# A planned single-core kernel: another order for the opening, and a last block that is scaled at eviction and fed from eleven weight-tile places

## The chip, the cores and the metric

The kernel runs on one core of one Trainium2 chip. The metric is the device time of one execution in microseconds (us), lower is better; the figure of a kernel is the median of its runs.

## The reference

Two model layers follow each other on 512 tokens of width 1024 (16 meta tokens stand ahead of them in the first), all in float32.

```python
# first_block: h = [meta; x], 528 rows
a = rmsnorm(h); aq, ak, av, rq, rf, ri, rg = split(a @ w_in)
att = diff_attention(aq, ak, av)    # rope, 4 heads, softmax(p0) - lam * softmax(p1), rmsnorm
rec = hgrn2(rq, rf, ri, rg)         # gated linear recurrence in chunks, rmsnorm, * silu(rg)
h = (h + [att, rec] @ w_out)[16:]
h = h + peer_ffn(rmsnorm(h))        # per token: 8 heads x top 16 of 16384 experts;
                                    # y = sum_k gelu(u[e_k] . x) * gate_k * v[e_k]
x = rmsnorm(h)
# second_block
q, k, v, z_a, u_b, v_b, z_b, g_a, g_b = split(rmsnorm(x) @ w_in_2)
y_a = stick_breaking_attention(q, k, v) * silu(z_a)      # 8 heads of 64
y_b = spatial_gating(gelu(u_b), gelu(v_b)) * silu(z_b)
x = x + (sigmoid(g_a) * (y_a @ w_up_a) + sigmoid(g_b) * (y_b @ w_up_b)) @ w_out_2
return rmsnorm(x)
```

The expert table is 16384 rows of 2048 floats (u and v of an expert together).

## The kernel before, in words

The tokens are four blocks of 128 rows, in partitions. Everything that any engine does is one list of steps, PLAN, made by make_plan from tables of rows written out by hand; each engine walks the same list and issues its own part of every step, so the order within an engine is the order of the list. Steps are named by a short name, the block or group of blocks, and a tile number: rf, rq, ak, aq, av, ri, rg are the seven projections of the first layer (four weight tiles each), n0/norm1 the norm and its transposes, fs/f/f2/lx/ly/lm/kd/ke/kdt/st the recurrence, us/ue/uw/ut/uv one attention head (scores, exponentials, weights, transposes, values), r1..r3 and a1..a3 the norm and transposes of the recurrent and the attention result, out the output projection. xn/xt/x2/x3, wq/sc/s1 and tk choose the experts. q2, k2, v2, vb, ub, zb, za, ga, gb, ua, ud, wo are the projections of the second layer, zs/zd/ze/zt/zv one unit of its attention, ln/l2/sg/yb the spatial gate, ya/yo/mt the transposes ahead of ua and wo, n1/m1/n2/n3 the two norms between the layers, fin/fd/store the last norm and the store.

Three parts follow each other. The opening (opening_rows, L155, and opening_keys) takes block 0 through the first layer's mixing up to its first experts. The middle is 256 ticks: POOL gathers 512 groups of 128 expert rows (1 MB each) into a ring of eight places, uv_rows; DVE multiplies them with the tokens (L1835), ACT takes gelu, DVE builds the weights (L1844, L1845) and PE adds the rows up in two PSUM banks, psum_y ("py"), the two halves of the tokens in output partitions 0-63 and 64-127. All other work of blocks 1 to 3 of the first layer and blocks 0 to 2 of the second is spread over these ticks. Behind the last tick last_rows (L245) takes block 3 through the second layer alone.

Weights come as tiles of 128 x 1024 floats (512 KB) in four places, wbuf. SP loads tile n into place n % 4 as soon as tile n - 4 was used (load_tile, L747 on); wherever a step uses a tile, SP's list has its load. PE matmuls are f32, and each is two instructions in the trace. Two rings of three PSUM banks, psum_a ("pa", emptied by ACT, semaphores a_full and a_free) and psum_b ("pb", emptied by DVE, b_full and b_free), take the results: cols_tile writes a projection transposed, rows_tile adds four tiles (16 instructions of 512 columns in the trace) into one bank per block. For block 0, rows_tile has a second bank for the 16 meta rows (`ps[0:NM, :]`), with as many instructions.

Around the last block: take_sums copies the two psum_y banks to h1 (L1851), n1 and m1 scale by the first layer's last norm (square, Ln and Exp on ACT, L1988 on DVE), n2 scales by the second layer's norm the same way, n3 transposes the rows (L895) and multiplies the columns by the norm's weights (L1589). Only then do q2 and k2 start, by cols_tile (L861). In opening_rows av stands behind us(0), rg behind us(2), and the eight steps of out at the very end:

```python
rows += [us(0), av, [("uw", b, 0)], [("ut", b, 0)], us(1), [("kdt", b), ("uw", b, 1), ("st", b)]]
rows += [[("uv", b, 0), ("ut", b, 1)], us(2), rg, [("r1", b), ("uw", b, 2)], [("uv", b, 1), ("ut", b, 2)], us(3)]
```

## Time and profile before

| | |
|---|---|
| median of 3 runs | 1992.65 us (1985.96 to 1992.9) |
| the profiled execution, its own time | 1989.25 us |
| its span, first to last instruction | 1987.5 us |
| busy in the span: PE, DVE, ACT, POOL | 1665.7, 1328.0, 653.7, 592.4 us |
| mean granted TensorE clock | 0.932 of 2.4 GHz |
| moved by DMA | 729.05 MB, mean 367 GB/s |

A row of instructions gives the start, the busy time (or the stretch from first to last start and end), engine, line, operation, what is written from what is read, and, in brackets, the idle time ahead of it with what ended it.

### The profile page before, as it was taken

How to read it: one execution, taken by the hardware profiler on the slowest of the kernel's cores; microseconds unless marked ns; L12 is line 12 of the kernel's file. 1: busy time of each engine (PE TensorE's matmuls, PEld its weight loads, DVE VectorE, ACT ScalarE, POOL GpSimd, SP SyncE). 2: the span in 40 equal slices, each digit the busy share in tenths (PEclk: the TensorE clock that was granted, in tenths of full speed). 3: DMA queues.
4: the chain of work that ended last, by engine and by line, in shares of the span. 5: the costliest groups of instructions: out<-in, count | busy, mean ns of one | idle time of the engine just before them, and what ended most of it. 6: DMA issues, size and time to landing. Idle time of an engine off the chain costs nothing.

```text
span 1987.5 us, 19846 instructions
## 1 busy us (share of the span) xinstructions
PE 1665.7 (84%) x6622; PEld 812.3 (41%) x6622; DVE 1328.0 (67%) x3461; ACT 653.7 (33%) x1219; POOL 592.4 (30%) x516
## 2 busy tenths in 40 slices
PE   7987798778898998788589999789986877876997
PEld 7445463225454443335145434333334222222653
DVE  4337787976788888875876578977656679644231
ACT  3123433323343265222231233511221246211361
POOL 0002233433232343533433233433323334421000
PEclk9988998889999998889899998899998988999999
DMA  7439999999999999999999999999999999998665
GB/s 219 133 120 367 417 417 417 421 417 417 397 402 356 352 413 360 353 420 414 421 416 417 418 416 372 356 411 418 419 403 362 417 412 409 419 417 344 212 222 180
DMA packets 130021, 729.05 MB, mean 367 GB/s; under 512 B 15600, under 2 KB 17264, under 8 KB 64384
## 3 DMA queue, kind: packets, MB, share of 16 engines
q0 software_dynamic: 73728, 536.90, 66.2%
q1 hardware_dynamic: 56192, 190.88, 25.8%
q8 instruction: 53, 0.87, 0.2%
q14 instruction: 48, 0.39, 0.1%
HBM read 725.63 MB, written 2.10 MB: 366 GB/s over the span
## 4 chain that ended last, share of the span: by engine, by line
PE 48%; DMA 23%; DVE 17%; ACT 5%; issue 5%; POOL 1%; POOLq 0%; DVEq 0%; SPq 0%; ACTq 0%
PE pa L861 27%; DMA uv_rows<-in_peer_uv,small 13%; PE py L861 12%; DMA wbuf<-in_wt 9%; PE pb L861 8%; DVE uv_rows L1835 6%; ACT area L1223 2%; ACT L1217 2%; POOL uv_rows L2025 1%; DVE tk L1845 1%; DVE area L1899 1%; DVE tk L1844 1%; DVE small L1822 1%; ACT small L1223 1%; DVE small L1740 1%
## 5 line engine op out<-in xcount | busy, mean ns | idle before, releaser
L2025 POOL DMA_INDIRECT uv_rows<-in_peer_uv,small x512 | 592.2, 1157 | 1214.5 <-PE py L861 968.3
L1835 DVE CUSTOM_DVE_ANT_0 uv_rows<-uv_rows,xrep 128x1024 f32<-128x1024 f32 x512 | 615.6, 1223 | 224.4 <-DMA uv_rows<-in_peer_uv,small 221.5
L861 PE MATMUL py<-uv_rows,tk 128*64 128x512 f32 x2048 | 568.9, 682 | 204.0 <-DVE tk L1845 203.3
L861 PE MATMUL pa<-wbuf,area 128*128 128x512 f32 (+2 forms) x864 | 383.8, 586 | 29.1 <-DMA wbuf<-in_wt 27.2
L1223 ACT ACTIVATE small<-small 128x2 f32<-128x2 f32 (+4 forms) x324 | 69.2, 214 | 847.4 <-DVE small L1835 823.6
L861 PEld LDWEIGHTS py<-uv_rows,tk 128*64 128x64 f32 x2048 | 136.5, 149 | 510.9 <-DVE tk L1845 277.6
L1217 ACT ACT_TABLE_LOAD x250 | 320.8, 1283 | 5.4 <-DVE small L1931 1.0
L861 PE MATMUL pa<-area,wbuf 128*128 128x128 f32 (+2 forms) x1408 | 249.3, 335 | 21.3 <-issue 11.1
L861 PEld LDWEIGHTS pa<-wbuf,area 128*128 128x128 f32 (+1 forms) x864 | 149.6, 189 | 254.5 <-issue 201.6
L861 PEld LDWEIGHTS pa<-area,wbuf 128*128 128x128 f32 x1408 | 215.9, 198 | 75.6 <-issue 41.7
L1223 ACT ACTIVATE area<-pa 128x512 f32<-128x512 f32 (+7 forms) x234 | 91.9, 409 | 310.4 <-PE pa L861 290.1
L861 PE MATMUL pb<-wbuf,area 128*128 128x512 f32 x352 | 164.8, 615 | 12.3 <-DMA wbuf<-in_wt 7.4
L1844 DVE TENSOR_TENSOR tk<-small 128x2 f32<-128x2 f32 x256 | 41.4, 162 | 104.0 <-issue 50.2
L861 PEld LDWEIGHTS pb<-wbuf,area 128*128 128x128 f32 x352 | 64.9, 194 | 111.6 <-issue 91.3
L861 PE MATMUL pa<-area 128*128 128x64 f32 (+7 forms) x392 | 77.9, 331 | 6.7 <-ACT area L1223 5.0
L1845 DVE TENSOR_TENSOR tk<-small,tk 128x128 f32<-128x128 f32 x256 | 74.8, 292 | 8.9
L861 PE MATMUL pb<-area 128*128 128x128 f32 (+7 forms) x434 | 77.4, 319 | 1.1 <-ACT area L1223 1.1
L1223 ACT ACTIVATE area<-area 128x512 f32<-128x512 f32 (+3 forms) x104 | 67.5, 655 | 26.8 <-DVE area L1631 18.8
L861 PEld LDWEIGHTS pa<-area 128*128 128x128 f32 (+2 forms) x392 | 54.1, 201 | 39.4 <-issue 23.0
L861 PEld LDWEIGHTS pa<-xnT,wbuf 128*128 128x128 f32 x512 | 59.3, 192 | 21.1 <-issue 16.5
L861 PE MATMUL pa<-xnT,wbuf 128*128 128x128 f32 x512 | 63.5, 280 | 2.2 <-DVE xnT L1589 1.1
L861 PEld LDWEIGHTS pb<-area 128*128 128x128 f32 (+2 forms) x434 | 54.9, 192 | 19.2 <-issue 13.9
(218 smaller groups left out, 1065.7 us busy)
## 6 DMA issues: line engine op xcount, KB each, us to landing
wbuf<-in_wt SPq DMA_DIRECT2D x336, 512.0 KB, 8.0
uv_rows<-in_peer_uv,small POOLq DMA_INDIRECT x512, 13.1
wbuf<-in_skT SPq DMA_DIRECT2D x11, 256.0 KB, 7.5
h<-in_x SPq DMA_DIRECT2D x4, 512.0 KB, 10.8
out<-h SPq DMA_DIRECT2D x4, 512.0 KB, 5.5
an<-in_x SPq DMA_DIRECT2D x3, 512.0 KB, 5.8
area<-in_finw SPq DMA_DIRECT2D x2, 512.0 KB, 10.0
area<-in_masks SPq DMA_DIRECT2D x1, 512.0 KB, 6.8
```

The costliest lines, as they stand in the source:

```text
L861: return nc.tensor.matmul(o, l, r, start=start, stop=stop, skip_group_check=True)
L1217: nc.scalar.preload_act_table_set(TABLES[func])
L1223: return nc.scalar.activation(dst, src, func, **more)
L1740: last = V.tensor_reduce(mx[:, q, part:part + 1], psum_a[(first + part) % RA][:, 0:nk - lo], AXX, ALU.max)
L1822: V.tensor_scalar(gate[to, cols], gexps[tok, g % 2, s_::TG], gsum[tok, g % 2, 1:2], None, ALU.mult)
L1835: last = V.tensor_tensor_reduce(uv_rows[:, n % RING, 0:D], uv_rows[:, n % RING, 0:D], xrep[:, b % 2, n % TG, :], 1.0, 0.0, ALU.mult, ALU.a ...
L1844: step(V.tensor_tensor(wcol[:, k % 2, :], dots[:, at:at + BATCH], gate[:, col:col + BATCH], ALU.mult))
L1845: V.tensor_tensor(mix_w[k % 2], token_mask.unsqueeze(1).broadcast_to([P, BATCH, TOK]), wcol[:, k % 2, :].unsqueeze(2).broadcast_to([P, BAT ...
L1899: step(V.tensor_tensor_scan(rcs[:, 0:wide][:, ::-1], seg2[:, 0:wide], soft[:, 0:wide][:, ::-1], 0.0, ALU.mult, ALU.add))
L2025: nc.gpsimd.indirect_dma_start(uv_rows[:, n % RING, :], None, t["peer_uv"], bass.IndirectOffsetOnAxis(ap=expert_ids[:, c:c + 1].bitcast(U3 ...
```

## The change

In the opening, the tiles of ri and av are taken in turn, and the meta rows of both go to one bank, ri's to partitions 0 to 15 and av's to 32 to 47 (first_rows). rg follows the first head's scores. out of block 0 adds straight into the two psum_y banks, first the tiles of the recurrent half (2, 3 of both column halves), later those of the attention half (0, 1), each when its columns are there; DVE adds the banks to h1. The twelve small constants and the masks are loaded from POOL's queue, once x has landed. In all heads of the first layer, the two parts' score products stand next to each other, and both banks are taken first.

In the last block, take, n1, m1, n2 and n3 are one step, hu: DVE multiplies each psum_y bank by the norm's weights, PE transposes it, and the unscaled columns go into the projections; ACT works out the two scales meanwhile and applies them at every eviction (last_s, last_s8). hx makes the scaled rows later. q2 and k2 become row projections, transposed behind (qt, kt); the scores of two heads are made together (zp) in two banks. The tiles have eleven places, four of wbuf and seven in the gather ring's memory; the first of them waits until the last gather has landed. mt and wo are cut in halves, the final norm and the store too. v2 stands ahead of the attention instead of in it.

```diff
-    rows += [aq[0:1], [("ly", b, 1)], aq[1:3], [("lx", b, 2), ("lm", b, 1)], aq[3:4], ri[0:1], [("ly", b, 2), ("rotq", g)]]
-    rows += [ri[1:2], [("lx", b, 3), ("lm", b, 2)], ri[2:3], [("ly", b, 3), ("kd", b)], ri[3:4], [("lm", b, 3), ("ke", b)]]
-    rows += [us(0), av, [("uw", b, 0)], [("ut", b, 0)], us(1), [("kdt", b), ("uw", b, 1), ("st", b)]]
-    rows += [[("uv", b, 0), ("ut", b, 1)], us(2), rg, [("r1", b), ("uw", b, 2)], [("uv", b, 1), ("ut", b, 2)], us(3)]
-    rows += [[("r2", b), ("uw", b, 3), ("r3", b)], [("uv", b, 2), ("ut", b, 3)], [("uv", b, 3)], [("a1", b), ("a2", b), ("a3", b)]]
-    return rows + [tiles("out", g, 0) + tiles("out", g, 1)]
+    rows += [aq[0:1], [("ly", b, 1)], aq[1:3], [("lx", b, 2), ("lm", b, 1)], aq[3:4], both(0), [("ly", b, 2), ("rotq", g)]]
+    rows += [both(1), [("lx", b, 3), ("lm", b, 2)], both(2), [("ly", b, 3), ("kd", b)], both(3), [("lm", b, 3), ("ke", b)]]
+    rows += [us(0), rg, [("uw", b, 0)], [("ut", b, 0)], us(1), [("kdt", b), ("uv", b, 0), ("uw", b, 1), ("st", b)]]
+    rows += [[("ut", b, 1)], us(2), [("r1", b), ("uv", b, 1), ("uw", b, 2), ("r2", b)], [("ut", b, 2)], us(3)]
+    rows += [[("r3", b), ("uv", b, 2), ("uw", b, 3)], out(0, 2, 3), [("ut", b, 3)], [("uv", b, 3)], out(1, 2, 3)]
+    return rows + [[("a1", b), ("a2", b), ("a3", b)], out(0, 0, 1), out(1, 0, 1)]
...
-    rows = [[("n1", b), ("m1", b), ("n2", b), ("n3", b)], tiles("q2", g) + tiles("k2", g)]
-    fill = [tiles(name, g) for name in ("v2", "vb", "ub", "zb", "za")]
+    rows = [[("hu", b)], tiles("q2r", g), tiles("k2r", g), [("qt", b)], tiles("v2", g), [("kt", b)]]
+    fill = [tiles(name, g) for name in ("vb", "ub", "zb", "za")]
...
-                row.append(("zs", *units[n]))
+        if n < n_units:
+            row += [("zp", b, n // 2)] * (n % 2 == 0) + [("zl", b, n)]
...
-    rows += [[("mt", b)], tiles("wo", g, 0), tiles("wo", g, 1), [("fin", b), ("fd", b), ("store", b)]]
+    for h in range(2):
+        rows += [[("mh", b, h)]] + [[("wo", g, c, 2 * h + i) for i in range(2)] for c in range(2)]
+    return rows + [[("fl", b)]]
...
+def places():
+    spots, nth, before, last, count = [], [], [], {}, {}
+    for n in range(len(LOADS)):
+        j = (n - TAIL) % (NW + XW) if n >= TAIL else 0
+        spot = j if j >= NW else (TAIL + j if n >= TAIL else n) % NW
...
+                elif SPOTS[n] >= NW:
+                    sp.wait_ge(uv_free, GATHERS - RING + 2 * BATCH)
+                if n == TAIL:
+                    sp.wait_ge(uv_full[RING - 1], 16 * (GATHERS // RING))
...
+            def first_rows(name, i):
...
+                if n:
+                    for k in range(2):
+                        rows_ = [mm(meta[32 * m:32 * m + NM, :], src[:, 2 * i + k, P:], first_tile[m][:, k, :],
+                                    i + k == 0, i == 3 and k == 1) for m in range(2)]
...
+                parts = [a_bank(), a_bank()]
+                for part, ps in enumerate(parts):
                     rows_ = slice(DH * part, DH * (part + 1))
-                    ps = a_bank()
                     mm(ps[:, 0:end - lo], q[rows_, hh, P * j:P * (j + 1)], kT[rows_, hh, lo:end], True, False)
+                for ps in parts:
                     mm(ps[:, end - lo - P:end - lo], ident, tri, False, True).then_inc(a_full, 1)
...
+            def paired_scores(b, pair):
...
+                banks = [b_bank(), b_bank()]
+                for part, ps in enumerate(banks):
+                    r = slice(DH2 * part, DH2 * (part + 1))
+                    mm(ps[:, :], q[r, pair, :], k2T[r, pair, :], True, False)
+                for ps in banks:
+                    mm(ps[:, W - P:], ident, stri, False, True).then_inc(b_full, 1)
...
+            def last_rows_up(b):
...
+                for c in range(2):
+                    if c == 1:
+                        dve.wait_ge(y1_read, 1)
+                    V.tensor_tensor(an[:, W * c:W * (c + 1)], psum_y[c][:, :], weights[:, W * c:W * (c + 1)], ALU.mult)\
+                        .then_inc(u_ready, 1)
+                weighted_columns(columns(hT_words, POST_OF[b]), P, normg2)
...
+            pool.wait_ge(ld_x[0], 16)
+            for name, dst in CONSTS:
+                pool.dma_start(dst, t[name]).then_inc(ld_c, 16)
+            pool.dma_start(masks.bitcast(I32), t["masks"]).then_inc(ld_k, 16)
```

How PE's order changes at three places. A row here is a run of like matmuls, each of which is two instructions in the trace; L861 and L919 are the helper that issues them, L965 and L1069 the transposes of the result rows, L993/L999 and L1098/L1104 those of a head's weights. First, the end of the opening on PE, before: two heads' values, the attention columns, and out into pb.

```order
61 L965 MATMUL pb<-ident,area 128x128 x4
62 L861 MATMUL pa<-area,uv_rows 128x128 x2
63 L993 MATMUL pa<-ident,uv_rows 16x128
64 L999 MATMUL pa<-ident,uv_rows 128x128
65 L861 MATMUL pa<-area,uv_rows 128x128 x2
66 L965 MATMUL pb<-ident,uv_rows 128x128 x4
67 L861 MATMUL pb<-wbuf,area 128x512 x16
```

The same place now, out into py:

```order
45 L1069 MATMUL pb<-ident,area 128x128 x4
46 L919 MATMUL pa<-area,uv_rows 128x128 x2
47 L919 MATMUL py<-wbuf,area 128x512 x4
48 L1098 MATMUL pa<-ident,uv_rows 16x128
49 L1104 MATMUL pa<-ident,uv_rows 128x128
50 L919 MATMUL pa<-area,uv_rows 128x128 x2
51 L919 MATMUL py<-wbuf,area 128x512 x4
52 L1069 MATMUL pb<-ident,uv_rows 128x128 x4
53 L919 MATMUL py<-wbuf,area 128x512 x8
```

Eight of the sixteen matmuls of out have moved ahead of the attention columns (the second group of transposes to pb), in two pieces between the last heads' steps.

Second, the start of the last block on PE, before: transposes, q2 and k2, the scores of one head and their mask, four tiles of v2.

```order
700 L895 MATMUL pb<-ident,an 128x128 x8
701 L861 MATMUL pa<-area,wbuf 128x128 x64
702 L861 MATMUL pb<-area 128x512
703 L861 MATMUL pb<-stri,ident 128x128
704 L861 MATMUL pa<-wbuf,area 128x512 x8
```

Now (L1301 are the unscaled transposes, L961 those of q and of k; tiles in uv_rows are the seven further places):

```order
662 L1301 MATMUL pb<-ident,an 128x128 x8
663 L919 MATMUL pa<-wbuf,area 128x512 x8
664 L919 MATMUL pa<-uv_rows,area 128x512 x8
665 L961 MATMUL pa<-ident,uv_rows 128x128 x4
666 L919 MATMUL pa<-uv_rows,area 128x512 x6
667 L919 MATMUL pa<-wbuf,area 128x512 x2
668 L961 MATMUL pa<-ident,uv_rows 128x128 x4
669 L919 MATMUL pb<-area 128x512 x2
670 L919 MATMUL pb<-stri,ident 128x128 x2
```

The 64 matmuls of 128 columns became 16 of 512 with eight transposes, v2 moved ahead of the scores, and two heads' scores stand together.

Third, the end on PE, before:

```order
747 L1090 MATMUL pa<-ident,area 128x128 x4
748 L861 MATMUL pb<-wbuf,uv_rows 128x512 x8
749 L895 MATMUL pa<-ident,uv_rows 128x128 x8
750 L861 MATMUL pb<-wbuf,area 128x512 x16
```

Now:

```order
709 L919 MATMUL pb<-wbuf,uv_rows 128x512 x2
710 L1206 MATMUL pa<-ident,area 128x128 x4
711 L919 MATMUL pb<-uv_rows 128x512 x8
712 L961 MATMUL pa<-ident,uv_rows 128x128 x4
713 L919 MATMUL pb<-uv_rows,area 128x512 x6
714 L919 MATMUL pb<-wbuf,area 128x512 x2
715 L961 MATMUL pa<-ident,uv_rows 128x128 x4
716 L919 MATMUL pb<-wbuf,area 128x512 x6
717 L919 MATMUL pb<-uv_rows,area 128x512 x2
```

The last piece of the gated product (two matmuls) now stands between the last head's values and the transposes of yo, and the transposes of merged rows and wo come in two halves.

## Rows read from the trace of the kernel before

**Rows 1.** Table of stretches, all engines: us, busy (count), PEclk, DMA share, GB/s.

```profile
0.00:163.00 163.00, 137.01 (x696) 92.91 (x697) 63.92 (x182) 42.97 (x110) 0.91 (x5) 0.94 0.52 166
163.00:1827.00 1664.00, 1390.44 (x5417) 643.28 (x5415) 1220.71 (x3223) 545.44 (x1003) 591.49 (x512) 0.93 0.99 403
...
1858.00:1951.00 93.00, 92.81 (x308) 47.08 (x308) 29.91 (x37) 52.65 (x80) 0.00 (x0) 1.00 0.70 230
```

**Rows 2.** Chain of waits in the last block: start us, us, what.

```profile
1859.73 6.87 PE pa L861 x16
1866.60 1.47 PE pb L861 x4
...
1947.69 3.50 PE pb L861 x8
...
1954.13 8.80 PE pb L861 x16
...
1966.35 14.16 PE pb L861 x32
```

**Rows 3.** Timeline of PE in the opening, ri and av.

```profile
52.30 3.70 PE L861 MATMUL pa<-wbuf,area 128*128 128x512 f32 x8
...
62.42 7.44 PE L861 MATMUL pa<-wbuf,area 128*128 128x512 f32 x16
...
75.42 14.98 PE L861 MATMUL pa<-wbuf,area 128*128 128x512 f32 x32 [1.87 <-ACT uv_rows L1223]
```

**Rows 4.** Timeline of all engines around and behind the last gather.

```profile
1817.74 40.44 SPq L759 DMA_DIRECT2D wbuf<-in_wt  x12
...
1826.88 1.23 DVE L1835 CUSTOM_DVE_ANT_0 uv_rows<-uv_rows,xrep 128x1024 f32<-128x1024 f32 x1 [2.54 <-DMA uv_rows<-in_peer_uv,small]
...
1828.93 1.94 PE L861 MATMUL py<-uv_rows,tk 128*64 128x512 f32 x8 [1.86 <-DVE tk L1845]
...
1830.98 1.29 DVE L1851 COPY h<-py 128x512 f32<-128x512 f32 x2 [1.51 <-PE py L861]
...
1838.30 1.97 PE L895 MATMUL pb<-ident,an 128*128 128x128 f32 x8 [7.44 <-ACT an L1223]
...
1841.12 16.70 PE L861 MATMUL pa<-area,wbuf 128*128 128x128 f32 x128 [0.85 <-DVE area L1589]
...
1983.13 1.28 DVE L2014 SCALAR_TENSOR_TENSOR h<-h,small,fw 128x1024 f32<-128x1024 f32 x1 [1.84 <-ACT small L1223]
```

**Rows 5.** Chain of waits at the end of the opening.

```profile
102.66 8.60 PE pa L861 x24
...
127.87 15.73 PE pb L861 x32
```

**Rows 6.** Table of stretches, PE alone: us, busy (count), PEclk, DMA share, GB/s.

```profile
118.00:128.00 10.00, 5.27 (x18) 0.50 0.00 0
```

**Rows 7.** Timeline of all engines in the opening.

```profile
7.48 1.04 ACT L1223 ACTIVATE area<-an 128x1024 f32<-128x1024 f32 x1
...
14.74 0.16 DVE L1571 TENSOR_TENSOR small<-small 128x4 f32<-128x4 f32 x1 [1.56 <-DMA small<-in_bs]
...
29.21 0.30 ACT L1223 ACTIVATE small<-small 128x8 f32<-128x8 f32 x2
...
164.92 0.93 POOL L2025 DMA_INDIRECT uv_rows<-in_peer_uv,small  x1 [0.30 <-issue]
```

**Rows 8.** DMA issues of the opening: KB each, median us to landing.

```profile
small<-in_bs SPq DMA_DIRECT2D x1, 4.0 KB, 4.2
```

**Rows 9.** Groups of PE instructions by form: count, busy us, mean ns, idle before.

```profile
L861 PE MATMUL pa<-area 64*128 64x400 f32 x16 | 7.5, 548 | 0.0
...
L861 PE MATMUL pa<-area 64*128 64x512 f32 x16 | 10.0, 704 | 5.0 <-ACT area L1223 5.0
```

**Rows 10.** DMA issues behind 1800 us: KB each, median us to landing.

```profile
wbuf<-in_wt SPq DMA_DIRECT2D x64, 512.0 KB, 4.5
```

**Rows 11.** Table of stretches of 25 us, all engines.

```profile
775.00:800.00 25.00, 21.30 (x90) 10.37 (x90) 21.28 (x61) 14.91 (x36) 8.06 (x6) 0.86 0.81 310
```

More of the change, by code:

```diff
@@ L47 @@
 NW = 4
+XW = 7
 TILE = KT * P
@@ L529, in build @@
         log08 = small.take(1)
-        ss = small.take(21)
+        ss = small.take(22)
         rs = small.take(21)
```

303 lines of the change are left out of this document (248 added, 55 removed).

## The prediction

> **What bounds the kernel now.** I read the table of stretches first, then the PE timeline of the opening and of the last block, then the chain of waits over both, and last the DMA share in between.
>
> The program has three parts [rows 1]. In the opening (to 163 us) DMA is busy only 0.52 of the time and PE for 137 of 163 us: PE and the short steps that PE waits for set the pace. From 163 to 1827 us DMA share is 0.99 at 403 GB/s: the expert gathers are bound by bytes, and PE (1390 of 1664 us) has room. After the last gather the last block runs alone: PE is busy 92.8 of 93 us from 1858 to 1951. So an edit is worth its price in the opening and behind the last gather, and next to nothing between.
>
> **The change, part by part.** The sum is made against the profiled execution's own 1989.25 us (span 1987.5 us), which lies 3.4 us under the median of 1992.65 us. A matmul is two instructions ("passes") in the trace; a pass of 512 columns takes 0.43 us (16 in 6.87 us [rows 2]).
>
> *Opening, ri and av.* These eight tiles take 64 passes: 3.70 + 3.70 + 7.44 + 14.98 = 29.8 us [rows 3] (the first row occurs twice). Half of them are for the 16 meta rows and cost as much as full ones. The change puts the meta rows of ri and av side by side at partitions 0 and 32 of one bank. The nearest row is the expert product: eight passes of 512 columns that alternate between two halves of the output partitions take 1.94 us [rows 4], not 8 x 0.43 = 3.4, so passes on different column groups run two at a time. With the meta pairs alike, 64 slots become 48: 22.4 us, -7.4. If groups of 16 do not pair: 0. I take -7.4, since the row is the same mechanism.
> The three banks must all be free before ri's first tile, one more than now; the third is freed by a copy after aq's last tile: +0.6 (bound 0).
> av no longer stands behind the first head's exponentials: rg's one bank is free at once, so the 1.87 us wait ahead of av [rows 3] goes: -1.9. What is late next is the state product, whose key transposes still need a bank from the second head.
> Four heads issue both halves of their scores next to each other (rows 0-63 and 64-127 of the array); if these pair, about 0.25 us each: -1.0 (bound 0).
>
> *Opening, out.* Today 32 passes stand at the end, 15.73 us [rows 5], the first ones at half clock: 0.50 is granted from 118 to 128 us [rows 6], in which PE did only 5.3 us of work. The change runs the recurrent half (16 passes, 6.9 us) inside that thin chain and leaves 16 passes behind the attention columns: 15.7 - 6.9 = -8.8. Cover for the moved half: from 111.3 us (102.66 + 8.60) to 127.87 us the chain is 16.6 us with little PE work [rows 5, 6]. Following the new order step by step I find the chain 1 us longer, and I charge 2.5 us for out passes that meet the half clock. Together -5.3 (bounds -9 and 0).
>
> *Opening, constants on POOL.* Twelve small loads and the masks leave SP's queue; a tile no longer stands behind the masks: -0.5. The new queue starts when x has landed, as ACT's first square does (7.48 us [rows 7]). POOL's cadence for a DMA is 1.24 us (0.93 busy and 0.30 of issue [rows 7]): 12 take until 22.4 us, and with the 4.2 us that a small load takes to land [rows 8] 26.6 us. DVE's sums for lambda start at 14.74 us today, are seven steps of some 0.2 us, and ACT takes them at 29.21 us [rows 7]: 28.2 us, just in time. Cost 0; without that 1 us of cover it is one for one, as the forget gates, and PE's first level product, follow.
> Opening: -7.4 + 0.6 - 1.9 - 1.0 - 5.3 - 0.5 = -15.5, and the gathers start that much earlier. Nothing stretches later, since the gathers are bound by bytes and the bytes stay.
>
> *Between.* In 12 heads of blocks 1 to 3 the two score products pair up, saving half of 5.8, 7.5 and 10.0 us of PE time (the last two in [rows 9], the first by their columns), 8 us counted in columns. Only where DMA falls short of full does that count: -2 (bounds -8 and +17, below).
>
> *Last gather.* The last block's first tiles are requested from 1817.74 us, while the last gather still runs; DVE gets it at 1826.88 us after waiting 2.54 us [rows 4]. The change holds them until that gather has landed. At most two tiles (1 MB at 403 GB/s, 2.6 us) stood in its way: -2 (bound 0). The held tiles then need 4.5 us [rows 10], and PE wants the first 4 + 2.7 us later: covered.
>
> *Start of the last block.* From the end of the last expert product (1828.93 + 1.94 = 1830.87 us) to the first projection (1841.12 us) pass 10.25 us: copy, square, roots, scaling, square, roots, scaling, transposes, columns [rows 4]. Now: one DVE product of a half (half of 1.29: 0.7), four transposes (half of 1.97: 1.0), one DVE column product (0.7), 0.3 of hand-overs = 2.7: -7.5. The seven small ACT steps of the scales end about 6 us in, the first eviction that needs them comes at 11.6 us: hidden.
>
> *q2 and k2 as rows.* Now 16.70 us [rows 4]. New: 32 passes, 13.7, plus 2 of cold start as now, plus two groups of transposes 0.9 = 16.6: 0. The scores wait 0.8 us for the key copy instead of 0.4, and the first wait for a tile (0.3) goes: 0.
>
> *Paired scores.* One head's two score passes and two mask passes take 1.47 us [rows 2], 1.07 of it columns. Two heads: 2.94 now; paired 0.86 + 0.43 + 0.4 for the two switches = 1.7. Four pairs: -5.0. Without pairing 2.55 each: -1.6. I take -5.0, by the column groups' row, though that is no row-group row.
> By the Trainium skill (TensorE: Matmul & The Clock Gate, "Packing small matmuls") tiles in different row groups run concurrently, which no row here shows. By TensorEngine Tiling (Array Packing), "Key Properties", a change of tiling mode drains the array, which speaks against frequent pairs; a price that would undo them is not given there.
>
> *Eleven places.* PE waits for a tile under 2 us in the whole last block, so more room is worth 0 (bound -1.5).
>
> *End.* From the last gated product (1947.69 + 3.50 = 1951.19 us) to the last matmul (1966.35 + 14.16 = 1980.51 us) 29.3 us pass, 8.80 us for 16 passes partly at the low clock among them [rows 2]. New: three times transposes, eviction and 16 passes, 0.45 + 0.75 + 6.87 = 8.07, together 24.2: -5.1. After it come 7.0 us to the end of the span (add, square, roots, scaling 1.28 at 1983.13 us [rows 4], store 3). In halves: 0.8 + 0.8 + 0.6 + 0.4, then 3 = 5.6: -1.4.
>
> Behind the last gather: -7.5 - 5.0 - 5.1 - 1.4 = -19.0. Sum: -15.5 - 2 - 2 - 19 = -38.5: 1950.7 us for the profiled execution, 1954 us beside the median.
>
> **Rivals.**
> *No pairing.* Neither 16-column nor 64-row groups overlap: +7.4 +1.0 +3.4 = 1966 us. Against it stands the 1.94 us row; for it, that row shows only 64-column groups. 0.13.
> *Banks taken in pairs.* The scores now wait for two free banks before their first pass, with the gathers' products queued behind them in PE's order. Block 3's already idle 5.0 us for ACT [rows 9]. Worst 1.4 us in each of 12 heads, 17 us; half of it: 1963 us. 0.12.
> *More between.* DMA falls to 0.81 in the stretch from 775 us [rows 11], and in a few like it; if PE held it there, all 8 us count: 1948 us. 0.13.
> *Slower: constants late.* At POOL's queue each DMA would have to take 1.24 + (1 + 38.5 + 10) / 12 = 5.4 us to turn the gain into a loss of 10 us: 2003 us. It decides from 4.6 us upwards; the rows say 1.24. 0.02.
> By the Trainium skill (DMA: Bandwidth & Descriptors, "SWDGE vs HWDGE vs iDMA") DMAs issued from GpSimd have their descriptors computed in software, while SP's are made in hardware and faster; its header gives about 1 us against 0.6 to the first byte, by which the constants would land 0.4 us later, still inside the cover.
>
> **How the numbers follow.** The forecast itself has 0.60. Half a per cent, 10 us, is about what a measurement of this kernel can tell from no change. Everything good at once (-19, -8, -2.5, -21.5) gives 1942 us; no pairing plus some of the bank waits gives 1968 us. Range 1942 to 1968. Faster by over 0.5% means under 1982.7 us, which fails only if the constants are late or two unknowns go wrong together: 0.95; within 0.5% 0.03; slower 0.02.
>
> **What would show it.** Right: av beside ri in about 5.2 us a pair; first gather issued some 15 us earlier; out's first half at the low clock, ending before the attention columns; 2.7 us from the last expert product to the first projection; 1.7 us a pair of heads; about 137 us from the last expert product to the end instead of 156.6. Wrong: a wait of DVE for the last constant after 28 us, a pair of heads at 2.5 us, a stretch between first and last gather over 1670 us (1664 now).

## The result, and the profile after

The changed kernel takes 1957.3 us (median of 4 runs, 1955.42 to 1959.62), the kernel before 1992.78 us (median of 4): a ratio of 0.983, 95% interval 0.9806 to 0.9855. That is 35.5 us less; 1954 was forecast, in a range of 1942 to 1968. The profiled execution took 1955.42 us with a span of 1953.6, so 33.9 us of span against the 38.5 of the sum. The sum came within 5 us, but three of its terms did not: the opening gave 3.1 us more than forecast, the middle gave nothing and the end only 1.0 us.

The table of stretches of the changed kernel, to be set against [rows 1] (us, busy (count) of PE, PEld, DVE, ACT and POOL, PEclk, DMA share, GB/s; the first two lines are the opening and the middle, the third is the part of the last block in which PE is full):

```profile
0.00:144.40 144.40, 124.41 (x693) 89.17 (x694) 64.03 (x183) 43.11 (x110) 8.49 (x18) 0.96 0.58 187
144.40:1809.50 1665.10, 1379.00 (x5420) 645.43 (x5418) 1220.92 (x3223) 545.91 (x1003) 591.51 (x512) 0.93 0.99 402
1832.00:1917.00 85.00, 84.11 (x299) 44.05 (x298) 29.91 (x37) 54.92 (x80) 0.00 (x0) 1.00 0.70 255
```

The opening is 18.6 us shorter (163.00 to 144.40), the middle is as long as it was (1664.00, now 1665.10) although PE has 11 us less to do in it, and the bytes per us are the same. Counted between events that both traces have, the 33.9 us are:

| from, to | before | after | change | forecast |
|---|---|---|---|---|
| start to first gather issued | 162.30 | 143.67 | -18.6 | -15.5 |
| to the end of the last expert product | 1668.57 | 1669.79 | +1.2 | -4 |
| to the first projection of the last block | 10.25 | 2.29 | -8.0 | -7.5 |
| to the last gated product's end | 110.06 | 103.80 | -6.3 | -5.0 |
| to the last matmul's end | 29.3 | 28.3 | -1.0 | -5.1 |
| to the end of the span | 7.0 | 5.8 | -1.2 | -1.4 |

PE's timeline in the opening of the changed kernel, where [rows 3, 5, 6] are now (start us, us, line, out<-in; L919 is the helper that issues products):

```profile
52.10 5.50 PE L919 MATMUL pa<-wbuf,area 128*128 128x512 f32 x16 [0.57 <-ACT area L1371]
...
58.49 5.42 PE L919 MATMUL pa<-wbuf,area 128*128 128x512 f32 x16
...
65.74 10.88 PE L919 MATMUL pa<-wbuf,area 128*128 128x512 f32 x32
...
93.18 3.57 PE L919 MATMUL pa<-area 128*128 128x128 f32 x16 [0.78 <-DVE area L1881]
...
105.80 5.72 PE L919 MATMUL py<-wbuf,area 128*128 128x512 f32 x8
...
112.99 3.60 PE L919 MATMUL py<-wbuf,area 128*128 128x512 f32 x8
116.45 0.65 PE L1069 MATMUL pb<-ident,uv_rows 128*128 128x128 f32 x4
117.96 7.13 PE L919 MATMUL py<-wbuf,area 128*128 128x512 f32 x16 [0.85 <-DVE area L1912]
```

ri and av take 5.50 + 5.42 + 10.88 = 21.8 us instead of 29.8. The 0.57 us ahead of them is a wait for ACT, which the trace of before does not have there: the third bank. The moved half of out is the two rows of eight passes, the first mostly at the low clock (5.72 us where the second takes 3.60), and what is left at the end takes 7.13 instead of 15.73 us.

The same view behind the last gather, to be set against [rows 2, 4]:

```profile
1811.52 1.94 PE L919 MATMUL py<-uv_rows,tk 128*64 128x512 f32 x8 [1.89 <-DVE tk L2056]
...
1814.31 1.32 PE L1301 MATMUL pb<-ident,an 128*128 128x128 f32 x8 [0.85 <-DVE an L2074]
...
1815.75 7.13 PE L919 MATMUL pa<-wbuf,area 128*128 128x512 f32 x16
...
1838.38 1.13 PE L919 MATMUL pb<-area 64*128 64x512 f32 x4 [0.89 <-ACT area L1371]
...
1839.44 0.71 PE L919 MATMUL pb<-stri,ident 128*128 128x128 f32 x4
...
1921.15 0.66 PE L1206 MATMUL pa<-ident,area 128*128 128x128 f32 x4 [1.60 <-DVE area L2258]
1922.49 8.83 PE L919 MATMUL pb<-uv_rows 128*128 128x512 f32 x16 [0.69 <-ACT uv_rows L1371]
1931.16 0.60 PE L961 MATMUL pa<-ident,uv_rows 128*128 128x128 f32 x4
1932.45 5.42 PE L919 MATMUL pb<-uv_rows,area 128*128 128x512 f32 x12 [0.69 <-ACT area L1371]
```

The chain of norms ahead of the first projection is one DVE product, transposes and columns: 2.3 us. Two heads' scores and masks stand in 1.6 us (1838.38 to 1839.99). The last rows show what the forecast of the end left out: PE waits 1.60 us for DVE ahead of yo's transposes, and behind them and a wait of 0.69 us for ACT, which the forecast had, 16 passes take 8.83 us, partly at the low clock, just as before.

### The profile page after: what moved, and what is told of

It is laid out like the page before. It is cut to its first block, busy times and chain, and to the rows that moved or that the text cites. A ratio compares the mean times of both kernels' runs of the same rounds, so it can differ in the third digit from the quotient of the medians.

```text
span 1953.6 us, 19684 instructions
## 1 busy us (share of the span) xinstructions
PE 1634.3 (84%) x6534; PEld 799.7 (41%) x6534; DVE 1328.8 (68%) x3466; ACT 656.3 (34%) x1224; POOL 600.0 (31%) x529
## 4 chain that ended last, share of the span: by engine, by line
PE 47%; DMA 23%; DVE 18%; ACT 5%; issue 5%; POOL 1%; POOLq 0%; DVEq 0%; SPq 0%; ACTq 0%
PE pa L919 26%; DMA uv_rows<-in_peer_uv,small 14%; PE py L919 13%; DMA wbuf<-in_wt 8%; PE pb L919 7%; DVE uv_rows L2046 6%; ACT area L1371 2%; ACT L1365 2%; POOL uv_rows L2291 1%; DVE tk L2056 1%; DVE area L2144 1%; DVE tk L2055 1%; DVE small L2033 1%; ACT small L1371 1%; DVE small L1951 0%
## 5 line engine op out<-in xcount | busy, mean ns | idle before, releaser
L919 PE MATMUL py<-uv_rows,tk 128*64 128x512 f32 x2048 | 560.8, 674 | 211.8 <-DVE tk L2056 208.1
L919 PE MATMUL pa<-wbuf,area 128*128 128x512 f32 (+2 forms) x784 | 342.0, 587 | 27.4 <-DMA wbuf<-in_wt 26.7
L919 PEld LDWEIGHTS py<-uv_rows,tk 128*64 128x64 f32 x2048 | 135.7, 148 | 514.6 <-DVE tk L2056 278.3
L919 PE MATMUL pa<-area,wbuf 128*128 128x256 f32 (+2 forms) x1280 | 233.7, 341 | 17.5 <-issue 12.0
L919 PEld LDWEIGHTS pa<-area,wbuf 128*128 128x128 f32 x1280 | 201.3, 199 | 70.6 <-issue 44.5
L919 PEld LDWEIGHTS pa<-wbuf,area 128*128 128x128 f32 (+1 forms) x784 | 134.2, 189 | 229.5 <-issue 176.5
L919 PE MATMUL pb<-wbuf,area 128*128 128x512 f32 x304 | 142.3, 612 | 11.1 <-DMA wbuf<-in_wt 7.3
L2055 DVE TENSOR_TENSOR tk<-small 128x2 f32<-128x2 f32 x256 | 41.7, 163 | 104.5 <-issue 51.7
L919 PEld LDWEIGHTS pb<-wbuf,area 128*128 128x128 f32 x304 | 55.8, 193 | 97.3 <-issue 81.7
L919 PE MATMUL pa<-area 128*128 128x64 f32 (+7 forms) x392 | 67.7, 345 | 13.7 <-ACT area L1371 12.3
L919 PE MATMUL pb<-area 128*128 128x128 f32 (+7 forms) x434 | 73.9, 321 | 1.6 <-ACT area L1371 0.9
L919 PEld LDWEIGHTS pa<-area 128*128 128x128 f32 (+2 forms) x392 | 51.2, 207 | 45.3 <-issue 35.3
L919 PEld LDWEIGHTS pa<-xnT,wbuf 128*128 128x128 f32 x512 | 60.2, 194 | 20.0 <-issue 16.4
L919 PE MATMUL pa<-xnT,wbuf 128*128 128x128 f32 x512 | 64.6, 282 | 2.0 <-DVE xnT L1800 1.1
L919 PEld LDWEIGHTS pb<-area 128*128 128x128 f32 (+2 forms) x434 | 53.9, 192 | 18.7 <-issue 12.6
```

The costliest lines, as they stand in the source:

```text
L919: return nc.tensor.matmul(o, l, r, start=start, stop=stop, skip_group_check=True)
L2055: step(V.tensor_tensor(wcol[:, k % 2, :], dots[:, at:at + BATCH], gate[:, col:col + BATCH], ALU.mult))
```

## The experiments

All start from the changed kernel. This table has the stages of each profile by the same events; the medians are of 4 runs, of 5 for e12 (before, on the same chips: 1990.69, 1991.03 and 1991.02).

| run | median us | first gather | middle | last expert product to last matmul |
|---|---|---|---|---|
| changed | 1957.3 | 143.7 | 1669.8 | 134.4 |
| e1_meta_apart | 1958.1 | 143.8 | 1672.4 | 134.4 |
| e2_scores_apart | 1972.4 | 145.8 | 1679.2 | 139.2 |
| e3_out_last | 1965.2 | 149.5 | 1673.5 | 134.1 |
| e4_no_hold | 1956.8 | 144.3 | 1672.0 | 135.7 |
| e5_meta_split | 1962.9 | 149.9 | 1669.7 | 134.4 |
| e6_scores_before | 1956.2 | 143.4 | 1669.3 | 134.2 |
| e7_end_whole | 1956.5 | 143.9 | 1672.5 | 133.9 |
| e8_heads_behind | 1966.4 | 145.6 | 1680.8 | 134.2 |
| e9_consts_sp | 1957.2 | 145.6 | 1671.1 | 132.7 |
| e10_four_places | 1956.7 | 143.9 | 1669.6 | 134.4 |
| e11_fill_last | 1956.1 | 144.0 | 1673.4 | 131.8 |
| e12_together | 1956.1 | 144.3 | 1676.8 | 130.9 |

How far the table can be read: the middle's order is the same in the changed kernel and in nine of the runs (all but e2, e6, e8), and it takes 1669.6 to 1676.8 us there. The opening is the same in the changed kernel, e4, e7, e8, e10, e11 and e12, and the first gather comes at 143.7 to 145.6. So 2 us in the opening and up to 7 in the middle prove nothing by themselves; the gather numbers and the timelines say more.

**e1, e5: does the overlap of ri's and av's meta rows need neighbours?**

In e1 ri's two meta matmuls (four passes) come first, then av's:

```diff
-                    for k in range(2):
-                        rows_ = [mm(meta[32 * m:32 * m + NM, :], src[:, 2 * i + k, P:], first_tile[m][:, k, :],
-                                    i + k == 0, i == 3 and k == 1) for m in range(2)]
+                    rows_ = [[mm(meta[32 * m:32 * m + NM, :], src[:, 2 * i + k, P:], first_tile[m][:, k, :],
+                                 i + k == 0, i == 3 and k == 1) for k in range(2)][1] for m in range(2)]
```

> The changed kernel, with the meta rows' matmuls of ri and av no longer alternating between the two column groups: in each pair of tiles both matmuls of ri come first, then both of av. Theory (two neighbours in PE's order on different column groups run at the same time, others don't): ri and av take 64 x 0.43 us or a little more, 27.5 to 29 us instead of 21.6, so the first gather starts 6 to 7 us later (150 us instead of 143.7) and the median is about 1964 us. Rival (any matmuls of the two groups that are near each other overlap, or the gain came from the shared bank): 21.6 us as now, first gather at 143.7 us, 1957 us.

PE's timeline of e1:

```profile
52.20 5.50 PE L919 MATMUL pa<-wbuf,area 128*128 128x512 f32 x16 [0.57 <-ACT area L1370]
```

The theory fell as stated: 5.50 us as with alternating passes. Within the row the eight meta passes start in pairs 13 ns apart, at 55.80, 56.24, 56.67 and 57.10 us (7 ns apart in the changed kernel), so av's first starts with ri's first although three of ri's stand ahead of it in the order. The rival of this experiment was vague, so e5 puts full-array passes between the groups, by issuing each tile's meta matmuls behind its own token rows:

```diff
-                if n:
-                    for k in range(2):
-                        rows_ = [mm(meta[32 * m:32 * m + NM, :], src[:, 2 * i + k, P:], first_tile[m][:, k, :],
-                                    i + k == 0, i == 3 and k == 1) for m in range(2)]
+                for k in range(2):
+                    last = mm(meta[32 * n:32 * n + NM, :], src[:, 2 * i + k, P:], first_tile[n][:, k, :],
+                              i + k == 0, i == 3 and k == 1)
```

> The changed kernel, with the meta rows' matmuls of ri issued straight behind ri's token rows and those of av behind av's, so that four passes on the whole array stand between the two groups of meta passes; the shared bank and the tile order stay. Theory (each column group takes its own passes one after the other at 0.43 to 0.46 us, and the array works on both groups at once whenever four passes of the one are followed by four of the other with nothing else between): no overlap is left, ri and av take 29 to 29.6 us instead of 21.6, the first gather comes 7 to 8 us later (151.3 us). Rival (the gain came from the shared bank or from the narrow product itself, not from an overlap): 21.6 us as now and the first gather at 143.7.

```profile
51.83 7.51 PE L919 MATMUL pa<-wbuf,area 128*128 128x512 f32 x16 [0.57 <-ACT area L1370]
```

With the same bank and the same tiles, 16 passes take 7.51 us again and all of ri and av 7.51 + 7.43 + 14.91 = 29.85 (before, 29.8). So neither the bank nor the narrow product made the gain: it is the overlap of column groups, and four passes of one group behind four of the other are near enough. The overlap is worth 8 us of PE's time and 6.2 us of the first gather (149.88 against 143.67). Most of the difference is the clock: the state product of 16 passes, 3.57 us in the changed kernel, takes 2.05 in e5.

**e2, e6: the first layer's score pairs**

In e2 both banks are taken first, but the order is score, mask, score, mask, in both layers:

```diff
                     mm(ps[:, 0:end - lo], q[rows_, hh, P * j:P * (j + 1)], kT[rows_, hh, lo:end], True, False)
-                for ps in parts:
                     mm(ps[:, end - lo - P:end - lo], ident, tri, False, True).then_inc(a_full, 1)
...
                     mm(ps[:, :], q[r, pair, :], k2T[r, pair, :], True, False)
-                for ps in banks:
                     mm(ps[:, W - P:], ident, stri, False, True).then_inc(b_full, 1)
```

e6 has in the first layer, on top of the first of these edits, one bank at a time, as in the kernel before:

```diff
-                parts = [a_bank(), a_bank()]
-                for part, ps in enumerate(parts):
+                for part in range(2):
+                    ps = a_bank()
```

> The changed kernel, with each score product followed by its own mask product again, in all heads of the first layer and in the last block; both banks are still taken first. Theory (gain is the overlap of the two half-array products and half of the changes between half-array and full-array products; no other place counts): each of the four heads of the opening takes 1.63 us instead of 0.99, first gather 2.6 us later; each pair of heads of the last block 2.7 us instead of 1.6, 4.4 us in all; the stretch from the first gather to the last expert product stays at 1670 us within 3 us although PE is busier in it; median 1964 us. Rival 1 (PE holds the stretches with a low DMA share): that stretch grows by some 8 us as well, 1972 us. Rival 2 (in the last block PE's order hid it): no change there, 1960 us.

> The changed kernel, with the first layer's scores as before in full: a bank is taken, its score and mask products follow, then the second bank. The last block keeps its pairs. Theory (taking both banks first costs what the pairing saves in block 3's heads: the second bank comes 2.4 to 4 us late from ACT and the first product used to run in that time): first gather 2 us later (145.8), gather 192 issued 638 to 640 us after the first instead of 648 in the run without pairs, the last expert product 1669 to 1672 us after the first gather; median 1959 to 1960 us. Rival (the 9 us of the run without pairs are a mere scatter of the middle, or come from PE's more busy time alone): the middle is as long as there, 1679 us, median 1968 us.

e2 settles the last block. PE's timeline of e2 there, one pair of heads; in the changed kernel the same takes 1.61 us:

```profile
1849.89 1.12 PE L919 MATMUL pb<-area 64*128 64x512 f32 x2 [0.89 <-ACT area L1369]
1850.94 0.49 PE L919 MATMUL pb<-stri,ident 128*128 128x128 f32 x2
1851.36 1.12 PE L919 MATMUL pb<-area 64*128 64x512 f32 x2
1852.41 0.49 PE L919 MATMUL pb<-stri,ident 128*128 128x128 f32 x2
1852.74 5.32 PE L919 MATMUL pa<-wbuf,area 128*128 128x512 f32 x12
```

2.85 us a pair, and 4.8 us more in the stage: row groups overlap too (four half-array passes in 1.06 us, two took 1.05). By the Trainium skill (TensorE: Matmul & The Clock Gate, "Packing small matmuls") tiles of different row groups run at the same time; this trace agrees.

The median says the same: 1972.4 us, 15 over the changed kernel. In the middle e2 lost 9 us and e6 lost nothing, though both have their products apart. Issue times of gathers on POOL, in us from the first:

```
gather      before   changed   e2      e6      e8
160         538.0    538.8     539.0   541.2   539.1
192         638.0    640.9     648.1   641.2   652.1
256         826.3    827.6     835.8   828.1   839.5
```

The loss falls on gathers 160 to 192, the stretch of low DMA share. They take 100.0 us before, 102.1 in the changed kernel, 109.1 in e2, 99.9 in e6 and 112.9 in e8; in the nine runs with the changed kernel's order they take 101.5 to 102.3. There PE works on block 3's heads. One head of e2, then the same of the changed kernel, then of e6 (x2 64*128 is a part's score product):

```profile
762.92 2.04 PE L919 MATMUL pa<-area 64*128 64x512 f32 x2 [4.00 <-ACT area L1369]
764.89 0.79 PE L919 MATMUL pa<-tri,ident 128*128 128x128 f32 x2
765.62 2.07 PE L919 MATMUL pa<-area 64*128 64x512 f32 x2
767.62 0.79 PE L919 MATMUL pa<-tri,ident 128*128 128x128 f32 x2
```

```profile
756.99 2.08 PE L919 MATMUL pa<-area 64*128 64x512 f32 x4 [4.00 <-ACT area L1371]
759.00 1.22 PE L919 MATMUL pa<-tri,ident 128*128 128x128 f32 x4
```

```profile
755.86 1.12 PE L919 MATMUL pa<-area 64*128 64x512 f32 x2
756.91 0.49 PE L919 MATMUL pa<-tri,ident 128*128 128x128 f32 x2
759.83 1.12 PE L919 MATMUL pa<-area 64*128 64x512 f32 x2 [2.43 <-ACT area L1370]
760.88 0.80 PE L919 MATMUL pa<-tri,ident 128*128 128x128 f32 x2
```

One bank at a time, the first part runs while ACT still empties the other bank. Both banks first, PE idles 4.0 us in one piece, and what follows runs at the low clock: the four passes of a part pair take 2.0 us, those apart 4.0. From the first score product to the product behind the masks pass 5.3 us apart (762.92 to 768.21) and 3.0 paired (756.99 to 760.01): the pair gets back 2.3 us a head. That is not all that the wait and the clock cost. From the start of the weights' transposes ahead of the scores to the product behind the masks this head takes 9.9 us in e2 (758.32 to 768.21), 7.6 in the changed kernel (752.40 to 760.01) and 6.1 in e6 (755.33 to 761.47).

Over the 32 gathers the numbers are alike: both banks first costs 9.2 us, the pairing gives back 7.0, and 2.2 stay lost. Over the whole middle that loss does not show (1669.3 us in e6, 1669.8 in the changed kernel); e6 comes to gather 160 some 2 to 3 us later than all the others, which was not followed up. e6's theory held for the length of the middle, but gather 192 came at 641.2 us and not at 638 to 640, and its 2 us of a later first gather did not come. So the two rivals "banks taken in pairs" and "more between" both held in the same place and about cancelled: by e6 the whole first-layer pairing is worth nothing that the totals show.

In the opening the timelines say more than the first gathers, which are within their scatter (143.4 us in e6, 145.8 in e2, 143.7 in the changed kernel). A head's scores and masks take 1.0 us paired and 1.6 apart. Taking both banks first costs the second head a wait of 0.56 us, in e2 as in the changed kernel, that e6 does not have. And the state product behind takes 3.57 us in the changed kernel, 2.05 in e2 and e6: with the scores apart it still runs at full clock.

**e8: the scores behind the expert product**

```diff
-        out += [("mix", k), *ticks[k], ("rows", k)]
+        heads = [s for s in ticks[k] if s[0] in ("us", "ue") and s[1] in (3,)]
+        out += [("mix", k), *[s for s in ticks[k] if s not in heads], ("rows", k), *heads]
```

> The changed kernel, with the score products of block 3's four heads in the first layer put behind the expert product of their tick instead of ahead of it. Theory (there PE waits 2.5 to 4 us for ACT's second bank with an expert product queued behind it that is ready, and the gathers starve for the places that this product frees): gather 192 is issued 3 to 10 us earlier than 641 us after the first, the DMA share of that stretch rises from 0.89, and the median falls by as much, to 1948 to 1954 us. Rival (the stretch is bound by the heads' own chain from scores to values, or the waiting moves to ACT and DVE): no gain, or some us lost, 1955 to 1962 us.

```profile
751.71 1.13 PE L920 MATMUL pa<-area 64*128 64x512 f32 x4
752.77 0.71 PE L920 MATMUL pa<-tri,ident 128*128 128x128 f32 x4
753.32 0.31 PE L920 MATMUL pa<-area 128*128 128x32 f32 x2
756.40 1.83 PE L920 MATMUL pa<-area 16*128 16x128 f32 x10 [2.78 <-ACT area L1372]
```

The theory fell: 9 us slower, and past the rival's 1962 too. In the head shown the scores run at full clock without a wait, but the next product (the head before's values) waits 2.78 us for a bank, until ACT has done its first exponentials of these scores (755.48 to 756.17 us); ACT itself came to them only after 4.23 us of waiting for DVE. Gather 192 comes at 652.1. So the stretch looks held by the head's chain between PE, DVE and ACT, in either order; no run isolates it, and a better order was not found here.

**e3: the moved half of out**

```diff
-    rows += [[("r3", b), ("uv", b, 2), ("uw", b, 3)], out(0, 2, 3), [("ut", b, 3)], [("uv", b, 3)], out(1, 2, 3)]
-    return rows + [[("a1", b), ("a2", b), ("a3", b)], out(0, 0, 1), out(1, 0, 1)]
+    rows += [[("r3", b), ("uv", b, 2), ("uw", b, 3)], [("ut", b, 3)], [("uv", b, 3)]]
+    return rows + [[("a1", b), ("a2", b), ("a3", b)], out(0, 2, 3), out(1, 2, 3), out(0, 0, 1), out(1, 0, 1)]
```

> The changed kernel, with the recurrent half of the opening's output projection no longer inside the chain of the last heads but directly behind the attention columns, still ahead of the attention half. Theory (the moved half was free, since PE had 7 us and more of idle time there; it costs a whole 16 passes at the end, some of them at the low clock): from the start of the third head's transposes to the start of the attention result's transposes 13.5 to 14 us instead of 14.4, the projection 14 to 16 us at the end instead of 7.1, first gather 7 to 8.5 us later, median 1965 us. Rival (moving it cost the chain what it saved behind it, through the low clock and PE's order): chain 3 us or more shorter, first gather at most 5 us later, 1961 us.

```profile
102.86 0.38 PE L1098 MATMUL pa<-ident,uv_rows 128*16 128x128 f32 x1 [2.15 <-ACT uv_rows L1371]
...
114.01 1.11 PE L1069 MATMUL pb<-ident,uv_rows 128*128 128x128 f32 x4 [3.30 <-DVE uv_rows L1900]
114.92 15.98 PE L919 MATMUL py<-wbuf,area 128*128 128x512 f32 x32
```

The first gather came 5.8 us later, between the two theories: from the third head's transposes to those of the attention result pass 11.15 us, against 14.4 with the half inside. So the half costs the chain 3.2 us (under 1 was expected in this experiment, 3.5 in the prediction) and takes 8.2 off the end (from the attention transposes to the end of out 8.64 us instead of 16.89; 8.8 in the prediction). The other 0.8 us of the 5.8 lie ahead of the chain, where nothing was changed (102.86 against 102.06 us). The net is 5.0 us, and the prediction's 5.3 was right.

The kernel before needed 14.0 us for the same chain (111.91 to 125.91) without any part of out, 2.9 us more than e3. That gain the prediction did not have. In the trace of before, PE waits 2.14 us in it for DVE ahead of the recurrent rows' transposes, and DVE comes to those rows only behind the fourth head's sums (116.06 us); in e3 it does them ahead of those sums (102.72 us), and PE does not wait there. So it comes from the new order of rg and of the recurrent steps; which of these, no run tells.

**e9: constants back on SP**

```diff
-            pool.wait_ge(ld_x[0], 16)
...
                 if s == ("rf", (0,), 3):
+                    for name, dst in CONSTS:
+                        sp.dma_start(dst, t[name]).then_inc(ld_c, 16)
...
+                elif s == ("rq", (0,), 3):
+                    sp.dma_start(masks.bitcast(I32), t["masks"]).then_inc(ld_k, 16)
```

> The changed kernel, with the twelve constants and the masks back on SP's queue, behind rf's and rq's last tiles as before. Theory (they landed in time before as they do now, at 14.7 us; only the tiles of rq and ak stood behind them, by 0.45 and 0.52 us): PE waits for tiles again for about 1 us in all in the first projections, the first gather comes 0 to 1 us later, the median stays within 1.5 us of 1957. Rival (the queue mattered more, since 13 loads of about half a microsecond each go ahead of tiles): first gather 3 us later or more.

The table of stretches for PE alone (us, busy (count), PEclk, DMA share, GB/s), first of the changed kernel, then of e9:

```profile
88.00:98.00 10.00, 8.33 (x52) 0.83 0.16 57
98.00:108.00 10.00, 7.72 (x33) 0.76 0.00 0
108.00:118.00 10.00, 8.63 (x25) 0.90 0.53 160
```

```profile
88.00:98.00 10.00, 8.33 (x44) 0.68 0.18 63
98.00:108.00 10.00, 7.72 (x37) 0.67 0.00 0
108.00:118.00 10.00, 9.49 (x22) 0.80 0.37 109
```

ri starts at 51.80 us, 0.3 before the changed kernel's 52.10 (51.7 to 52.6 in the other runs), so the queue itself is worth nothing: PE waited 1.35 us for one tile, at 27.5 us, and made it good. The first gather is 1.9 us later all the same, and the lines show where: with the same instructions in the same order the granted clock is lower from 88 to 118 us. The constants are not the reason: e8, whose opening is the changed kernel's, has 0.70, 0.67 and 0.78 in the same stretches and its first gather at 145.6 us. The expected median was met.

**e4: no hold on the last tiles**

```diff
-                if n == TAIL:
-                    sp.wait_ge(uv_full[RING - 1], 16 * (GATHERS // RING))
```

> The changed kernel without the wait that holds the last block's weight tiles until the last gather has landed. Theory (the last gathers are not slowed by a megabyte or two of other traffic, since they landed 3.7 us apart with and without it): the last expert product ends within 0.5 us of where it does now, counted from the first gather (1669.8 us), the last block's start and length stay, 1957 us. Rival (my term: the tiles stand in the last gather's way): 2 to 5 us later, since up to eleven tiles may now be asked for before it, 1960 us. Third: the tiles were late in the changed kernel, and the last block gets shorter by up to 1 us.

DVE's use of the last two gathers, of the changed kernel, where the tiles are asked for from 1809.52 us, and of e4, from 1802.16:

```profile
1805.76 1.23 DVE L2046 CUSTOM_DVE_ANT_0 uv_rows<-uv_rows,xrep 128x1024 f32<-128x1024 f32 x1 [1.75 <-DMA uv_rows<-in_peer_uv,small]
1809.47 1.23 DVE L2046 CUSTOM_DVE_ANT_0 uv_rows<-uv_rows,xrep 128x1024 f32<-128x1024 f32 x1 [2.48 <-DMA uv_rows<-in_peer_uv,small]
```

```profile
1807.49 1.23 DVE L2044 CUSTOM_DVE_ANT_0 uv_rows<-uv_rows,xrep 128x1024 f32<-128x1024 f32 x1 [1.78 <-DMA uv_rows<-in_peer_uv,small]
1811.21 1.23 DVE L2044 CUSTOM_DVE_ANT_0 uv_rows<-uv_rows,xrep 128x1024 f32<-128x1024 f32 x1 [2.48 <-DMA uv_rows<-in_peer_uv,small]
```

3.71 and 3.72 us apart: the hold does not bring the last gather earlier. The middle as a whole is 2.2 us longer, within what it varies by itself. The last block is 1.3 us longer: PE is still at the low clock there, with the last expert product at 2.98 us instead of 1.94 and the first 16 passes behind at 8.04 instead of 7.13, and no wait for a tile. The medians are equal (1956.8 and 1957.3). No gain of the hold is seen.

**e10: four places**

```diff
-XW = 7
+XW = 0
```

> The changed kernel with four places for the last block's weight tiles instead of eleven; the first of them still waits for the last gather. Theory (PE's use of a tile takes 1.7 us and a tile's load 4.5 us, with three more under way, so four places nearly keep up and DMA is the bound only in the first rows): the stretch from the last expert product to the last matmul grows from 134.4 by 1 to 5 us, all of it in waits for tiles of 1 us or less, mostly in the first 30 us; median 1959 to 1962 us. Rival 1 (my prediction: worth nothing, since PE waited under 2 us for tiles before): below 1 us. Rival 2 (a load can only be asked for once PE has left its place, and the queue then runs dry for the whole block): 10 us or more.

```profile
1832.00:1917.00 85.00, 84.11 (x299) 44.00 (x297) 29.89 (x37) 54.85 (x80) 0.00 (x0) 1.00 0.74 244
```

PE's line is that of eleven places to the digit, and PE waits for no tile in the whole block. The prediction's 0 was right, and my 1 to 5 us of this experiment wrong.

**e7, e11, e12: the end**

e7, e11 and what e12 adds to both:

```diff
-    for h in range(2):
-        rows += [[("mh", b, h)]] + [[("wo", g, c, 2 * h + i) for i in range(2)] for c in range(2)]
+    rows += [[("mh", b, 0), ("mh", b, 1)], tiles("wo", g, 0), tiles("wo", g, 1)]
```

```diff
-    fill += [tiles(name, g, c) for name in ("gb", "ga") for c in range(2)]
-    fill += [[("ud", g, 0, i) for i in range(2)], [("ud", g, 1, 0)], [("ud", g, 1, 1)]]
+    fill += [tiles("gb", g, 0), tiles("gb", g, 1), tiles("ga", g, 0), [("ud", g, 0, 0)]]
+    fill += [[("ud", g, 0, 1), ("ud", g, 1, 0)], [("ud", g, 1, 1)], tiles("ga", g, 1)]
```

```diff
-    rows = [[("hu", b)], tiles("q2r", g), tiles("k2r", g), [("qt", b)], tiles("v2", g), [("kt", b)]]
+    rows = [[("hu", b)], tiles("q2r", g), tiles("k2r", g), [("qt", b), ("kt", b)], tiles("v2", g)]
```

> The changed kernel, with both halves of the merged rows transposed first and the last output projection in whole columns (eight tiles in the old order); the final norm's two halves stay. Theory (the halves only hide one hand-over from DVE and split the projection; most of the 29.3 us of before were never in their reach): from the last gated product to the last matmul 29.3 us instead of 28.3, the median within 1.5 us of 1957. Rival (my prediction's term: the halves are worth 5.1 us): 33 us there, median 1962 us.

> The changed kernel, with the last gate's four tiles (ga, second half) issued behind the last head's values instead of three heads earlier, and the products of ud moved forward by one to three heads. Theory (PE's 1.6 us of waiting ahead of the transposes of yo, and the 1.7 us that the next projection loses at the low clock, have no cover; 16 passes give it): no wait ahead of yo's transposes, ua's 16 passes in 7.1 instead of 8.8 us, the last heads not later: the last expert product to the last matmul 131 to 132 us instead of 134.4, median 1954 to 1955 us. Rival (the last two heads' exponentials and transposes need the cover that is taken from them, or ACT comes to yo later behind the gate's table load): the gain is given back, 134 us or more.

> The fill of the run before, the last projection in whole columns, and the key transposes ahead of v2 instead of behind it, together. Theory: 2.5 us from the fill, 0.5 from whole columns and 0.4 from the scores' wait for the key copy (0.9 us now): the last expert product to the last matmul about 131 us, median about 1953.5 us, faster than both kernels. Rival (the heads lose what the fill gains): 134 us and 1957 us.

e7: from the last gated product to the last matmul 27.8 us instead of 28.3, where its theory had 29.3 and its rival 33. So it is worth nothing, or half a microsecond the wrong way, to issue half of wo between the two groups of transposes. The merged rows still come in two steps in e7, and PE waits 1.17 us for DVE there, against 1.60 and 0.74 us for ACT before. e11, PE's timeline:

```profile
1917.30 7.09 PE L919 MATMUL pa<-wbuf,area 128*128 128x512 f32 x16
1924.22 0.60 PE L1206 MATMUL pa<-ident,area 128*128 128x128 f32 x4
1925.64 7.13 PE L919 MATMUL pb<-uv_rows 128*128 128x512 f32 x16 [0.83 <-ACT uv_rows L1371]
```

The wait ahead of yo's transposes is gone and the projection runs in 7.13 us: the stage is 2.6 us shorter (131.8), and 3.4 in e12 (130.9), as expected. The totals don't show it: medians 1956.1 both, with the middle 3.6 and 7.0 us longer in the profiles. Of the changed kernel and e12 the ratios to before are 0.983 (0.9806 to 0.9855) and 0.9825 (0.9808 to 0.9842). A version that beats the changed kernel is thus shown in its last stage, and not in its time.

## Why the prediction was right, point by point

- **Opening, ri and av.** Right in mechanism and size: -8.0 of PE's time for -7.4, shown by e5, of which 6.2 reach the first gather. Third bank +0.57 for +0.6. The wait ahead of av is gone.
- **Opening, scores.** -1.0 was forecast. Against the old order it is 0 as far as can be told (e6). The overlap is there, 0.6 us a head, but the step counted it alone: the second head's wait for banks (0.56 us) and the low clock of the state product (1.5 us) take it back.
- **Opening, out.** -5.3 forecast, 5.0 measured (e3), with its parts about as charged (3.2 of chain and low clock for 3.5, 8.2 off the end for 8.8).
- **Opening, constants.** 0 by e9. Their cover was 12.3 us and not 1: POOL issues most of its plain loads 0.54 us apart, not 1.24 as its gathers, DVE's sums for lambda start at 14.76 us as before and end at 16.4, and ACT comes for them at 28.62. The rival "constants late" had no ground.
- **What the opening's sum lacked:** 2.9 us in the chain of the last heads, from the new order of rg and the recurrent steps (the trace of before against e3; neither was moved back by itself).
- **Between.** -2 forecast, and the middle did not shorten. That a cut of PE's time there may count was right (e2: 9 us, more than the 8 of the rival; the heads shown run at the low clock). That the bank wait takes it back was the other rival. The prediction gave them as alternatives; both happen, in the same heads.
- **Last gather.** -2 forecast, no gain measured (e4). The step that failed is "at most two tiles stood in its way": the last gathers are 3.7 us apart with no other load under way, and 3.8 before.
- **Start of the last block.** -8.0 for -7.5, with 2.3 us for 2.7. No run undid it; it rests on the two traces.
- **q2 and k2.** 0 forecast; from the first projection to the first scores, less v2's 6.9 us, 15.8 us instead of 17.1: -1.3. The 2 us of cold start that I kept went with the idle time ahead, 16 passes in 7.13 us.
- **Paired scores.** -5.0 forecast; 1.61 us a pair, 4.8 us by e2. Counted from start to start, one head took 1.37 us before and not 1.47, so against the kernel before it is 4.5 us.
- **Eleven places.** 0 and 0 (e10).
- **End.** -5.1 forecast, -1.0 measured: the largest miss. "Three times transposes, eviction and 16 passes" left out PE's 1.60 us for DVE ahead of yo's transposes and the low clock of the 16 passes behind (1.7 us), both inside the old 29.3 us, the second in [rows 2]; e11 removes these two and gets 2.6 us. The halves, on which the step's idea rested, gained nothing by e7.
- **Final.** -1.2 for -1.4.

The misses are +3.1 in the opening's favour and 5.2, 4.1 against it in the middle and the end, partly made good in the last block. That the total still came within 3 us of the forecast is in part luck.

## What to carry to other kernels

Before pairing two products, ask what the first of them was doing while the second's buffer was still occupied: taking both buffers first turns that overlap into one long wait, and the clock falls behind it. A split at the end only pays for waits that it really covers; list the idle times of the stage first and ask of each one whether the edit touches it (here 1.6 and 0.7 us were in plain sight). And where a stage varies by up to 7 us between profiles of the same order, judge a 3 us edit by its own stage, and say that the total doesn't show it.

## What the runs showed of the hardware

- Passes on two column groups overlap although four of one are issued ahead of four of the other (e1: 16 passes in 5.50 us, of which eight at 0.43 us are full-array ones, so that the eight narrow ones take 2.0 us). With full-array passes between them they don't (e5: 7.51 us).
- The granted clock depends on more than the idle time just ahead. The projection ua stands behind the same waits, 1.60 and 0.69 us, in the changed kernel and in e9, with the same rows of the last block ahead of them, and takes 8.83 us in the one (shown above) and 7.13 in the other:

```profile
1925.64 7.13 PE L923 MATMUL pb<-uv_rows 128*128 128x512 f32 x16 [0.69 <-ACT uv_rows L1375]
```

- The last gathers do not come at the rate of the middle (402 GB/s, DMA share 0.99). With no tile load under way, 1 MB lands every 3.7 us, and the share and rate of DMA in the changed kernel fall to:

```profile
1803.46:1808.46 5.00, 4.40 (x14) 1.73 (x15) 1.69 (x4) 0.03 (x1) 0.00 (x0) 1.00 0.69 279
```

What holds them was not tried.
